# Differential attention: the scores of a step on four groups of 32 rows, in place of stationary tiles with zero rows

## The reference, cut to what matters

```
s = jnp.einsum('bqhcd,bkhcd->bhcqk', q, k, preferred_element_type=F32) * (A_QK ** -0.5)
p = jax.nn.softmax(s, axis=-1)
a = p[:, :, 0] - lam * p[:, :, 1]
return jnp.einsum('bhqk,bkhd->bqhd', a.astype(v.dtype), v)
...
s_win = jnp.einsum('brqhd,brikhd->brhqik', qg, k_rows, preferred_element_type=F32) * scale + bias
s_ctx = jnp.einsum('brqhd,bkhd->brhqk', qg, kc, preferred_element_type=F32) * scale
p = jax.nn.softmax(jnp.concatenate([s_win, s_ctx], axis=-1), axis=-1)
```

## Time and profile before

| | us |
|---|---|
| three runs: lowest, median, highest | 2427.86, 2428.32, 2429.92 |
| the profiled execution | 2428.85 |
| its span, first to last instruction | 2427.0 |
| the stage of the change in it | from about 256 to 421 |
| PE busy over the span | 2283.8 (94%) |

### The profile page before, as it was taken

One profiled execution on the slowest core, in us unless ns is written; L12 is line 12 of the kernel. 1 busy time (PEld: TensorE's weight loads), 2 busy tenths in 40 slices (PEclk: granted clock), 3 DMA queues, 4 the chain that ended last, 5 costly groups with the idle time before them and its releaser, 6 DMA issues.

```text
span 2427.0 us, 28782 instructions
## 1 busy us (share of the span) xinstructions
PE 2283.8 (94%) x10062; PEld 1606.8 (66%) x10063; DVE 978.6 (40%) x1800; ACT 540.9 (22%) x1133; POOL 188.1 (8%) x181
## 2 busy tenths in 40 slices
PE   8999899867798998999999999999999999999999
PEld 2554455422333477778888888566676788888888
DVE  5532688530000135725335432444244534335421
ACT  3201466411111144522111100131231212111100
POOL 0000436011111000000000002202010000000000
PEclk9999999878899999989999999999999999999999
DMA  9220153559787921012222221312112122222230
GB/s 350 84 97 30 43 189 136 231 192 381 270 334 261 353 107 52 27 53 78 87 86 82 75 104 54 129 44 86 61 60 78 35 105 79 88 87 89 75 120 19
DMA packets 81023, 298.02 MB, mean 123 GB/s; under 512 B 8989, under 2 KB 8989, under 8 KB 80430
## 3 DMA queue, kind: packets, MB, share of 16 engines
q1 hardware_dynamic: 75102, 271.26, 31.7%
q0 software_dynamic: 5840, 25.67, 2.9%
HBM read 282.73 MB, written 14.16 MB: 122 GB/s over the span
## 4 chain that ended last, share of the span: by engine, by line
PE 84%; DVE 7%; issue 3%; ACT 3%; SPq 2%; DMA 2%; DVEq 0%; POOL 0%; ACTq 0%; POOLq 0%
PE products L1589 41%; PE products L988 8%; PE products L1419 6%; PE products L1212 6%; PE products L1494 3%; PE products L1437 3%; PE products L1753 2%; PE products L1671 2%; PE products L1328 1%; PE products L1544 1%; DVE tiny L2531 1%; PE products L1227 1%; SPq L828 1%; DMA weights_and_work<-in_experts 1%; ACT weights_and_work L1960 1%
## 5 line engine op out<-in xcount | busy, mean ns | idle before, releaser
L1589 PE MATMUL products<-normed,weights_and_work 128*128 128x264 f32 (+1 forms) x1520 | 348.7, 384 | 0.0
L1589 PEld LDWEIGHTS products<-normed,weights_and_work 128*128 128x128 f32 x1520 | 288.1, 190 | 50.7 <-issue 5.3
L1419 PE MATMUL products<-weights_and_work 128*64 128x512 f32 x768 | 181.1, 632 | 47.3 <-DMA weights_and_work<-in_experts 46.6
L1589 PE MATMUL products<-weights_and_work,mixed 128*128 128x256 f32 (+1 forms) x800 | 182.3, 382 | 0.8 <-ACT weights_and_work L1844 0.8
L1844 ACT ACTIVATE weights_and_work<-products 128x256 f32<-128x256 f32 (+4 forms) x225 | 99.4, 456 | 371.5 <-PE products L1589 156.4
L1419 PEld LDWEIGHTS products<-weights_and_work 128*64 128x64 f32 x768 | 65.6, 146 | 161.1 <-issue 160.0
L1589 PEld LDWEIGHTS products<-weights_and_work,mixed 128*128 128x128 f32 x800 | 151.8, 190 | 24.4 <-ACT weights_and_work L1844 1.6
L1589 PE MATMUL products<-weights_and_work 128*128 128x256 f32 (+1 forms) x672 | 151.0, 386 | 7.2 <-DVE residual L3248 5.2
L1589 PE MATMUL products<-weights_and_work,normed 128*128 128x264 f32 (+1 forms) x704 | 155.6, 382 | 0.0
L1589 PE MATMUL products<-normed,mixed 128*128 128x264 f32 (+1 forms) x672 | 154.1, 382 | 0.0
L1589 PEld LDWEIGHTS products<-weights_and_work 128*128 128x128 f32 x672 | 128.9, 192 | 28.0 <-issue 7.3
(11 more groups left out here) (565 smaller groups left out, 2974.0 us busy)
## 6 DMA issues: line engine op xcount, KB each, us to landing
weights_and_work<-in_weights SPq DMA_DIRECT2D x301, 512.0 KB, 4.3
weights_and_work<-in_experts SPq DMA_DIRECT2D x192, 512.0 KB, 5.3
results<-normed SPq DMA_DIRECT2D x8, 512.0 KB, 7.1
residual<-in_x POOLq DMA_DIRECT2D x1, 2048.0 KB, 15.7
weights_and_work<-in_dft_half POOLq DMA_DIRECT2D x1, 2048.0 KB, 13.3
token_rows<-mixed SPq DMA_DIRECT2D x4, 512.0 KB, 3.1
normed<-results SPq DMA_DIRECT2D x4, 512.0 KB, 7.1
mixed<-results SPq DMA_DIRECT2D x4, 512.0 KB, 8.6
```

The source lines that it names most:

```text
L1419: m = pe.matmul(ps[UNIT * b:UNIT * (b + 1), side, :], job_t[:, k, UNIT * b:UNIT * (b + 1)], expert_w[b][:, s, at:at + 512], start=(k == 0) ...
L1589: m = pe.matmul(bank(p, n), left(k), right(k), start=(fresh and k == 0), stop=(k == kt - 1), skip_group_check=True)
```

## The change

The zero-padded copies are gone, with the memset, ACT's copies and their semaphores. Every product of scores now takes 32 rows of the queries and of the keys as they lie. The 32 components of A's set 0, of its set 1, and the two halves of B are four groups of rows; B's two halves are added up in PSUM, the first with `start`, the second without. There are ten products a step instead of six: widths 256, 512, 512, 256, 512, then 256, 256, 256, then 256. Two groups never write one bank at once by this order: PE waits for its own results on `halfway` before it writes the banks that another group has used, and on `ending` before the last product. A and B are reported together by that last product, and PE waits for the banks of both before it begins.

```diff
@@ -501,8 +501,6 @@
         scaled_b = arena[:, 12032:12032 + NKEY]
         prob_t = piece(arena, 12800, 2, NKT, P)
         o_root = arena[0:DH, 22520:22520 + HEADS * P]
-        aq_alone = piece(arena, 8192, 2, 2, P)
-        bq_alone = piece(arena, 8704, 2, P)
         raw_a = piece(mix[:, :, :].rearrange("p k t -> p (k t)"), 0, 4, S)
         part_out = [arena[:, a:a + S] for a in [14336 + S * m for m in range(5)] + [23032] + [21496, 21496 + S]]
         acc2 = piece(h_flat, 2 * D, 4, TILE)
@@ -637,7 +635,7 @@
         mod1_ready = sem("mod1_ready")
         conv_ready, spec_ready, folded = sem("conv_ready"), sem("spectrum_ready"), sem("signal_folded")
         roped, pooled = sem("roped"), sem("pooled")
-        q_zeroed, q_alone = sem("lone_queries_zeroed"), sem("queries_alone")
+        halfway, ending = sem("scores_halfway"), sem("scores_ending")
         max_a, max_b, prob_ready, b_ready = sem("max_a"), sem("max_b"), sem("prob_ready"), sem("prob_b_ready")
         prob_scaled = sem("prob_a_scaled")
         bias_set, lam_arg, lam_exp = sem("bias_set"), sem("lam_arg"), sem("lam_exp")
@@ -960,10 +958,10 @@
                 for b, v in p.after:
                     pe.wait_ge(bank_free[b], plus(v, p.free_step, it))
 
-            def finish(p, ins):
+            def finish(p, ins, n=1):
                 assert p.order == made[0], (p.order, made[0])
-                made[0] += 1
-                ins.then_inc(done, 1)
+                made[0] += n
+                ins.then_inc(done, n)
 
             def weights(name, i, it=None):
 
@@ -1220,20 +1218,34 @@
                         return
                     t, h = STEPS[s]
                     a, b_ = r["scores", s, "A"], r["scores", s, "B"]
+                    o = DH * (h % 2)
                     fill(a)
-                    pe.wait_ge(q_alone, s + 1)
-                    for c in range(2):
-                        for at, width in ((0, 512), (512, 256)) if c == 0 else ((0, 256), (256, 512)):
-                            m = pe.matmul(wide(a, 2 * NKEY)[:, NKEY * c + at:NKEY * c + at + width], aq_alone[:, h % 2, c],
-                                          ak[:, h // 2, at:at + width], start=True, stop=True)
-                            if s == 0 and c == 0 and at == 0:
-                                begin(m)
-                    finish(a, m)
                     fill(b_)
-                    for at, width in ((0, 512), (512, 256)):
-                        m = pe.matmul(wide(b_, NKEY)[:, at:at + width], bq_alone[:, 1 - h % 2], bk[:, h // 2, at:at + width],
-                                      start=True, stop=True)
-                    finish(b_, m)
+
+                    def product(to, at, q, k, row, key, width, start=True, stop=True):
+                        rows_ = slice(row, row + 32)
+                        return pe.matmul(to[:, at:at + width], q[rows_, h // 2, t * P:(t + 1) * P], k[rows_, h // 2, key:key + width],
+                                         start=start, stop=stop)
+
+                    def first(c, key, width):
+                        return product(wide(a, 2 * NKEY), NKEY * c + key, aq, ak, o + 32 * c, key, width)
+
+                    def second(half, key, width, start, stop):
+                        return product(wide(b_, NKEY), key, bq, bk, DH - o + 32 * half, key, width, start, stop)
+
+                    first(1, 0, 256).then_inc(halfway, 1)
+                    m = first(0, 0, 512)
+                    if s == 0:
+                        begin(m)
+                    second(0, 0, 512, True, False).then_inc(halfway, 1)
+                    second(1, 512, 256, True, False).then_inc(halfway, 1)
+                    first(1, 256, 512).then_inc(ending, 1)
+                    pe.wait_ge(halfway, 3 * s + 3)
+                    first(0, 512, 256).then_inc(ending, 1)
+                    second(1, 0, 256, False, False)
+                    second(0, 512, 256, False, True).then_inc(ending, 1)
+                    pe.wait_ge(ending, 3 * s + 3)
+                    finish(a, second(1, 256, 256, False, True), 2)
 
                 def turn(s, kind):
                     pe.wait_ge(prob_ready if kind == "A" else b_ready, s + 1)
@@ -1927,23 +1939,7 @@
                 for i in range(2):
                     copy(r["pool"][i], pool_u[:, i, 8:8 + S], bank(r["pool"][i]))
                 for t in range(NKT):
-                    if t == NKT - 2:
-                        act.wait_ge(q_zeroed, 1)
-                        act.wait_ge(roped, 2)
-                        read(act, r["bq"][1])
-                        for s in range(2):
-                            alone(s)
                     copy(r["v"][t], vals[:, t], bank(r["v"][t]).rearrange("p (a c) -> p a c", a=2))
-
-            def alone(s):
-
-                t, h = STEPS[s]
-                at, o = slice(t * P, (t + 1) * P), DH * (h % 2)
-                for c in range(2):
-                    rows_ = slice(o + 32 * c, o + 32 * c + 32)
-                    act.activation(aq_alone[rows_, h % 2, c], aq[rows_, h // 2, at], ACT.Copy)
-                rows_ = slice(DH - o, 2 * DH - o)
-                act.activation(bq_alone[rows_, 1 - h % 2], bq[rows_, h // 2, at], ACT.Copy).then_inc(q_alone, 1)
 
             def attentions():
 
@@ -1993,9 +1989,6 @@
                 for s in range(len(STEPS)):
                     if s - 1 in SUMMED_AT:
                         sums(SUMMED_AT[s - 1])
-                    if s + 2 < len(STEPS):
-                        read(act, r["scores", s, "B"])
-                        alone(s + 2)
                     exps(s + 1, "A")
                     if s > 0:
                         weighed(s - 1)
@@ -2500,7 +2493,6 @@
                         link(tt_(mean, mean, pool_inv[o:o + DH, i], ALU.mult))
                         ins = tt_(pool_y[o:o + DH, i], mean, pool_u[o:o + DH, i, 8:8 + S], ALU.subtract)
                     ins.then_inc(pooled, 1)
-                dve.memset(arena[:, 8192:8960], 0.0).then_inc(q_zeroed, 1)
                 link(dve.tensor_tensor_scan(lane, ones, ones, -1.0, ALU.mult, ALU.add))
                 link(dve.tensor_reduce(partition, con("earlier"), AX_X, ALU.add))
                 link(ts(partition, partition, -1.0, float(P - 1), ALU.mult, ALU.add))
```

## The result

The changed kernel takes **2438.4 us** (median of 7 runs, 2432.6 to 2440.7) where the kernel before took 2428.9 beside it (7 runs, 2426.2 to 2429.9): a ratio of 1.0036 with an interval of 1.0025 to 1.0048 (the two medians alone give 1.0039). It is slower by a third of a per cent. The prediction of 2426.1 and its range up to 2437 both missed it. Among the runs of the kernel before that stand beside x1 to x4 one took 3065.07 us, and no ratio counts it. The profiled execution of the changed kernel took 2435.3 us with a span of 2433.5, so it is 6.5 above that of before (2427.0), and its split is read from here on. The median lies another 3.1 us higher, and no trace shows those. The four runs from 2438.4 us up have a mean granted clock of 0.964 over the program where the profiled one has 0.966; that fits with more time at half clock and does not show it.

A forecast was written before the change was run, and what follows sets the result against it. The prediction took a ring through PE, DVE and ACT, 9.3 us an ordinary step, as the bound; eight steps at 0.28 us gave 2.2 us off, all else nothing: 2426.1 us, range 2422 to 2437.

The forecast's parts named there:

- The clock: Rival: more PE idle in the attention stage halves its clock, 1.5 to 1.9 us of passes a fall; chance 0.20.
- the ring: Ordinary step's chain of scores A, maxima, exponentials, last transposes and output pieces through PE, DVE and ACT: 9.3 us.
- five or six: Count of clock falls in the attention stage said to make the kernel 8 us slower, 2436.
- 0.28 us per step on the path: Scores A in eight ordinary steps: predicted to end this much earlier, 2.2 us off in all.
- two waits of 0.27: PE's waits for its own results between the three score phases: tail 0.166, waking 0.04, load 0.06 each.
- A wait of 0.4: Sign of being wrong: a wait showing 0.4 us or more between the score phases.
- The rule that I set aside: Changing tiling mode drains the array; one tail per entry to the scores would leave 0.11 a step, 2427.4.
- The rest of the change, at nothing: ACT copies, DVE memset, early copies, new wait for exponential B and added increments: counted as no time.
- exponential B: Scores newly wait for the step before's exponential B; 0.9 us of cover. Rival that it bites: 2431, chance 0.03.
- The later wait, of step 1: Scores of step 1 wait about 2 us for exponential B, said to be hidden by 4.0 us.
- the rivals of two groups and of none: Score products overlap only two at a time (2436, chance 0.12) or not at all (2466, chance 0.03).
- the steps paced by DVE: Later steps, six besides step 1, where DVE is behind: said to gain nothing from earlier scores.

The follow-up runs named there:

- x1: The kernel before with one edit: PE waits for B's banks ahead of A's scores; 2429.53 us, ratio 1.0005.
- x4: The kernel before plus one wait of PE for its own result between the two matrices of A; 2429.24 us, ratio 1.0008.
- x3: The changed kernel plus three idle full-width products a step, ahead of A's first four transposes, read by nobody; 2429.11 us, ratio 1.0011.
- x11: x2 plus the three idle products a step of x3; 2429.90 us, ratio 1.0010.
- x2: The changed kernel with the wait for B's banks moved behind A's first two products; 2433.20 us, ratio 1.0030.
- x9: x3 with one idle product a step instead of three; 2429.87 us, ratio 1.0015.
- x8: x7 plus the three idle products a step of x3; 2435.28 us, ratio 1.0029.
- x7: x5 with B as two whole products of 64 rows instead of five of 32 that add up; 2432.76 us, ratio 1.0017.
- x12: x11 with ACT's three copies a step put back, read by nobody; 2429.14 us, ratio 1.0009.
- x5: The changed kernel with A's four products first and handed over by a semaphore of their own, ahead of B's end; 2421.96 us, ratio 0.9973.
- x6: x5 plus the three idle products a step of x3; 2423.53 us, ratio 0.9980.

## Why the prediction was wrong

**The clock, which I gave a chance of 0.20, was the largest part.** The rival stood in the text with its place and its price: PE's idle to 1.9 us, 1.5 to 1.9 us for a fall. Both came about (1.88; 1.3 to 1.7 for a fall). What failed is the weight. The trace before showed half clock after 3.81 us of idle and none after 1.74. I took the gap between for open, leaned to the good side, and put the clock into the sum at nothing. But 1.74 was a long idle among steps whose idle was 0.58; after the change no step from 280 us on has less than 1.88. That the falls came with the work taken from PE, and made most of the loss, is shown by x3 against the changed kernel, by x11 against x2, and by the clock of x3, x9 and x11 (1.00 from 280 us on): work was added, the ring stayed at 9.48, the falls went, and some 6 us with them. What exactly brings a fall is not shown: in x8 one came behind no idle at all, and in x1 one came without the small products. Why a fall struck the step at 342 us and not its neighbours, which look alike, stays open; runs of the changed kernel spread over 8 us, and my count of "five or six" for 2436 took 2.2 us of gain off, which did not exist.

**"0.28 us per step on the path" had the wrong sign.** The term was 2.56 against 1.71 of passes and two waits of 0.27, with nothing or 0.08 at the entry. The 1.71 was right: four groups ran at once. From the first load at 295.68 to the end of the last pass at 297.82 + 0.67 it is 2.81 us; less 1.71 of passes, 0.17 of tail and 0.10 of opening load, 0.83 is left for two waits, 0.41 each. The parts: tail 0.17, load 0.10 where I had 0.06, waking 0.11 to 0.17 where I had 0.04. I had read load and waking from full-width products that wait for ACT; the wait of PE for itself among 32-row groups was in no row, and x4 gives 0.32 even for full width. The entry cost another 0.20: the first load begins 0.10 after the last full-width pass has streamed (294.72 + 1.02 - 0.17 = 295.57 to 295.68), and 0.10 of that load is in sight. I had taken 0.03 for it (0.31 to 0.28). So 2 x 0.14 and 0.17 more than I had, 0.45, turn 0.28 off into 0.17 on; measured are 0.16. A wait of 0.4 stood in the text as a sign of being wrong, but no bound of the sum was made from it.

The rule that I set aside bears on this. The Trainium skill (TensorEngine Tiling (Array Packing), Key Properties) says that changing the tiling mode drains the array. I answered that the 64-column groups of L1256 start 0.07 before the passes of L1234 end. That was too quick: 0.07 is less than the tail of 0.17, and in going from 128 to 32 rows the trace now shows 0.10 of gap. x7 agrees with the rule more plainly, with 32- and 64-row products that never overlap. The estimate from the rule, a tail of 0.17 more at each entry, is about what the entry cost above my figure; the dearer waits are the other part of the error.

**"The rest of the change, at nothing" overlooked step 0.** I looked for what B's banks wait for in later steps (exponential B, rightly hidden) and not for who holds them when the stage starts. It is DVE's second pool copy: 0.94 us in sight, 1.0 on the first maxima. The later wait, of step 1, I had hidden behind 4.0 us of cover. That cover was used up (the last pass ended at 270.73, the maxima began at 270.76), as PE idled 5.98 us there and the scores then ran at half clock; in x1 it did not suffice. x1 shows the wait of step 0 in the kernel before with that one line; x2 that it can't be had back by moving the line, while A is handed over last.

**Right:** the four groups overlap fully, the rivals of two groups and of none are out. The ring and the steps paced by DVE are as they were read. ACT's copies cost nothing that shows (x12). Exponential B holds the scores in step 1 alone and was just hidden there. The list of what PE idled for ahead of L1227 in the changed kernel (us, times):

```profile
  ACT weights_and_work L1956: 6.0, 1
  DVE mixed L2512: 0.9, 1
```

A fall costs about what was said.

**What the change could have given.** Its passes would let A end sooner; it gives the gain away by handing A over with B, behind two waits. x5 keeps the four groups and releases A after its own four products: 2421.96, 0.27% below before.

## What to carry to other kernels

When small products are packed to take load off an engine that waits in a ring, price each wait of PE for itself at 0.3 to 0.4 us and the entry into the small tiles at 0.2, and hand over the result that the ring waits for with a semaphore of its own, ahead of the one that nobody waits for (x5). Then ask what PE's freed time does to its clock: if idle grows in every turn of a loop, look at the granted clock in the stage before reading anything else into the time, and try one idle product in the gap: if the time falls and the ring stays, the clock was the cause (x9). Where PE itself is the path it only costs (x6, x8). And when a wait is moved forward, look at its first turn apart, since other work holds the buffer there.

## What the runs showed of the hardware

Four fp32 products of 32 rows by 128 columns on different row groups start within 0.02 us and stream side by side at full rate, each with its two passes (a pass of 512 columns takes 0.43 us of columns, as at full width). Products of 32 and of 64 rows on different rows did not run together: three meetings a step in x7, each one behind the other. A wait of PE for itself costs 0.32 us among full-width products (x4) and about 0.41 among 32-row ones. With idles of 1.88 to 3.03 us in every step the clock fell to half four times; with 1.40 to 1.89 us in the same places it stayed at 1.00 (x9). Idle time alone does not tell: with 1.25 us in the ordinary step it fell twice (x7), and once behind 20 us without any (x8).
